# Sums of squares of a norm: channel groups added on VectorE in fp32 ahead of one column-sum matmul per half

## The reference

```python
def rms_norm(x, g):
    xf = x.astype(jnp.float32)
    y = xf * lax.rsqrt(jnp.mean(xf * xf, axis=-1, keepdims=True) + EPS)
    return (y * g.astype(jnp.float32)).astype(x.dtype)

h = modulate(rms_norm(x, g_ffn1), sh1, sc1);  x = x + 0.5 * gt1 * swiglu(h, w_ffn1_in, w_ffn1_out)
h = modulate(rms_norm(x, g_mix), sh2, sc2);   x = x + gt2 * token_mix(h, ...)
h = modulate(rms_norm(x, g_ffn2), sh3, sc3);  x = x + 0.5 * gt3 * swiglu(h, w_ffn2_in, w_ffn2_out)
```

## Time and profile before

| what | us |
|---|---|
| median of three runs | 1582.96 (1581.0 to 1584.09) |
| the profiled execution, its own time | 1581.47 |
| its span on the slowest core (spans of all: 1572.1 to 1579.6) | 1579.6 |
| TensorE matmul busy | 1494.0 (95%) |
| VectorE busy | 809.4 (51%) |
| ScalarE busy | 454.8 (29%) |
| GpSimd busy (it issues the weight loads) | 78.4 (5%) |
| chain that ended last, on TensorE | 88% of the span |

### The profile page before, as it was taken

How to read it: one execution, slowest core, us unless ns; L and a number is a source line. 1 busy time by engine, 2 the same in 40 slices (tenths; PEclk the granted TensorE clock), 3 DMA queues, 4 the chain that set the end, 5 groups by cost and what they waited for, 6 DMA issues and landing times.

```text
span 1579.6 us, 23368 instructions; the slowest of 8 cores (1572.1 to 1579.6 us)
## 1 busy us (share of the span) xinstructions
PE 1494.0 (95%) x8372; PEld 707.3 (45%) x8372; DVE 809.4 (51%) x1315; ACT 454.8 (29%) x641; POOL 78.4 (5%) x152
## 2 busy tenths in 40 slices
PE   1597999999999999988999999999999999999998
PEld 1243444444444444454565444444444444444443
DVE  1353717245163556667875557745544616253644
ACT  2462010110101026548666444523511010101010
POOL 1001000000000000000000000001000000000000
PEclk7799999999999999999999999999999999999999
DMA  9946142531624201340024445336332131211022
GB/s 176 249 84 94 29 71 47 88 67 28 107 54 74 41 14 67 76 103 1 15 68 73 76 68 121 68 64 116 54 54 40 28 54 28 47 27 28 1 107 107
DMA packets 24302, 107.12 MB, mean 68 GB/s; under 512 B 2816, under 2 KB 3072, under 8 KB 21760
## 3 DMA queue, kind: packets, MB, share of 16 engines
q0 software_dynamic: 21312, 75.67, 28.7%
q1 hardware_dynamic: 2880, 29.98, 5.4%
HBM read 168.71 MB, written 12.58 MB: 115 GB/s over the span
## 4 chain that ended last, share of the span: by engine, by line
PE 88%; DMA 6%; DVE 2%; ACT 2%; issue 2%; POOL 0%; DVEq 0%; ACTq 0%; POOLq 0%
PE ps L663 42%; PE ps L693 21%; PE ps L1007 7%; PE ps L817 4%; PE ps L1020 3%; PE ps L1039 3%; DMA arena<-w1i 2%; PE ps L953 1%; DMA arena<-w_kqvu 1%; PE ps L800 1%; PE ps L577 1%; DMA arena<-w_ada 1%; DVE arena L496 1%; PE ps L899 1%; PE ps L863 1%
## 5 line engine op out<-in xcount | busy, mean ns | idle before, releaser
L663 PE MATMUL ps<-arena 128*128 128x512 bf16 x3152 | 690.7, 380 | 7.8 <-DMA arena<-w1i 4.9
L484 ACT ACTIVATE arena<-ps 128x512 bf16<-128x512 f32 (+3 forms) x426 | 268.0, 653 | 967.1 <-PE ps L663 800.7
L663 PEld LDWEIGHTS ps<-arena 128*128 128x128 bf16 x3152 | 306.7, 98 | 376.9 <-issue 12.1
L496 DVE SCALAR_TENSOR_TENSOR arena<-ps,arena 128x512 f32<-128x512 f32 (+1 forms) x500 | 359.5, 747 | 79.0 <-PE ps L693 20.4
L490 DVE TENSOR_TENSOR arena<-arena,ps 128x512 bf16<-128x512 bf16 x198 | 134.7, 686 | 501.0 <-PE ps L663 482.4
L693 PE MATMUL ps<-arena 128*128 128x512 bf16 x1584 | 346.7, 380 | 5.9 <-DMA arena<-w1o 3.8
L693 PEld LDWEIGHTS ps<-arena 128*128 128x128 bf16 x1584 | 155.1, 98 | 194.1 <-issue 11.9
L490 DVE TENSOR_TENSOR arena<-arena 128x1024 bf16<-128x1024 bf16 (+8 forms) x178 | 109.9, 637 | 33.6 <-ACT arena L484 27.6
L1007 PE MATMUL ps<-arena 128*128 128x512 bf16 x512 | 116.0, 379 | 0.0
L496 DVE SCALAR_TENSOR_TENSOR arena<-arena 128x512 f32<-128x512 f32 (+1 forms) x120 | 84.4, 739 | 31.5 <-ACT arena L484 22.2
L484 ACT ACTIVATE arena<-arena 128x512 f32<-128x512 f32 (+2 forms) x86 | 89.5, 1053 | 35.7 <-DVE arena L496 22.8
(11 more groups left out here) (60 smaller groups left out, 495.5 us busy)
## 6 DMA issues: line engine op xcount, KB each, us to landing
arena<-w_ada POOLq DMA_DIRECT2D x36, 512.0 KB, 8.9
arena<-w_gate POOLq DMA_DIRECT2D x24, 512.0 KB, 7.3
arena<-w1i POOLq DMA_DIRECT2D x22, 512.0 KB, 7.1
arena<-w3i POOLq DMA_DIRECT2D x22, 512.0 KB, 5.2
arena<-x SPq DMA_DIRECT2D x5, 2048.0 KB, 14.1
outT<-arena SPq DMA_DIRECT2D x8, 1024.0 KB, 3.9
arena<-w1o POOLq DMA_DIRECT2D x10, 512.0 KB, 6.7
arena<-w_kqvu POOLq DMA_DIRECT2D x10, 512.0 KB, 7.9
```

Source lines behind the costliest of these rows:

```text
L484: return e.activation(out=o, in_=i, func=func, scale=scale)
L496: return e.scalar_tensor_tensor(out=out, in0=in0() if callable(in0) else in0, scalar=scalar, in1=in1() if callable(in1) else in1, op0=op0, ...
L663: ins = e.matmul(pst(t), lhsT=w[:, kt, :], rhs=hk(b, kt), start=(kt == 0), stop=(kt == 7))
```

## The change

`norm_stats` gets `sub` as an argument. ScalarE squares as before. For each half, VectorE adds the first two channel groups to the other two (bf16 in, fp32 out, 128 x 1024) into `pair`, which lies on the same bytes as the two buffers of `TMPS`; then it adds the two parts of `pair` (128 x 512) and writes bf16 into one of the two `SQK` buffers. TensorE then sums that over channels with one matmul per half, two per norm in place of eight. `kq_unit` takes the buffers of `SQK` in the same rotation, which now starts with the norms.

```diff
+    PAIRS = [view(o, F32, (2, TB)) for o in (o_qt, o_expb)]
...
     rk_pos = [0]
+    sqk_pos = [0]
     tmp_pos = [0]
 
-    def norm_stats(b):
+    def norm_stats(b, sub):
         t = Tile()
         for hf in range(2):
             sq = H[:, b, 4 * hf:4 * hf + 4, :]
             xs = xblk(b)[:, 4 * hf:4 * hf + 4, :]
             act(sq, xs, AF.Square, reads=[xs], writes=[sq], cost=1.88)
+        pair = PAIRS[0 if sub < 2 else 1]
         for hf in range(2):
-            sq = H[:, b, 4 * hf:4 * hf + 4, :]
-
-            def mm(e, hf=hf):
-                ins = None
-                for kt in range(4 * hf, 4 * hf + 4):
-                    ins = e.matmul(pst(t), lhsT=ONES, rhs=hk(b, kt), start=(kt == 0), stop=(kt == 7))
-                return ins
-            S.op("pe", mm, reads=[sq, ONES] + ([t] if hf else []), writes=[t], cost=mmc(4, 512))
+            sm = SQK[sqk_pos[0] % 2]
+            sqk_pos[0] += 1
+            lo, hi = H[:, b, 4 * hf:4 * hf + 2, :], H[:, b, 4 * hf + 2:4 * hf + 4, :]
+            tt(pair, lo, hi, ALU.add, [lo, hi], [pair], 1.15)
+            tt(sm, pair[:, 0, :], pair[:, 1, :], ALU.add, [pair], [sm], 0.62)
+            S.op("pe", lambda e, hf=hf, sm=sm: e.matmul(pst(t), lhsT=ONES, rhs=sm, start=(hf == 0), stop=(hf == 1)),
+                 reads=[sm, ONES] + ([t] if hf else []), writes=[t], cost=mmc(1, 512))
...
     def norm(b, sub):
-        norm_apply(b, sub, norm_stats(b))
+        norm_apply(b, sub, norm_stats(b, sub))
...
-    rs0 = norm_stats(0)
+    rs0 = norm_stats(0, 0)
...
-    sqk_pos = [0]
```

## The result

The changed kernel takes 1596.51 us (median of four runs, 1593.28 to 1599.22) against 1582.47 for the kernel before on the same chip (1581.0 to 1584.09). The ratio is 1.0089, with a 95% interval of 1.0072 to 1.0106: some 14 us slower. In some executions the cores of a die run at a lower granted clock (on one chip the kernel before took 1744 to 1869 us in them); every ratio here leaves these out. The forecast was 1577, 5.2 us faster by its sum, with a range up to 1587.

The account below looks back on a forecast made before the run. The prediction took mostly busy TensorE as the bound, the end moving with the second feed-forward step's start. Stages summed to -0.5 + 1.8 + 3.9 = 5.2 us earlier, 1577.8 on the median's scale, put at 1577; range 1566 to 1587.

Parts of the forecast that it names:

- What a norm costs and what it gives back: All norms: VectorE adds 3.83 us per norm, 53.6 in all; TensorE saves 1.3 per norm, ceiling 18.1.
- Sub 2: Stage 1004 to 1124 us: norm 1 gives 0, norms 2 to 4 give 1.3 each, 3.9 us earlier.
- Wait (2): Sub 2: the pair lies in the bias table, last read long before these norms' sums; no cost.
- Sub 1 up to the keys: Stage 561 to 687 us: norms 0 and 3 give 1.3 each, norm 2 loses 0.8; 1.8 us earlier.
- The stage of sub 0: 0 to 154 us: taken as 0.5 us later, bounds 5.2 earlier and 4.2 later.
- wait (1): Pair on `TMPS` bytes: a norm's first add waits for the previous norm's last temporary to be read; unit products wait too.
- the "+0.1": Sub 0, norm 2: 1.4 us later at the Silu batch, less 1.3 for norm 3's sums following at once.
- slower by the shared bytes: Rival: in five norms of sub 0 and 1 waiting adds block unit products, 12.7 us lost, 1588; chance 0.11.
- "Norm 4: ... 0": Sub 1, norm 4: its sums stand between a load's issue and the wait for it at 686.83; 0 gain.
- "no change, since priorities stay": 687 to 1004 us, where no norm runs: the planner reorders everything, but no change in time was taken.
- Wait (3): Key and query squares share `SQK` with the norms, but already waited for the last norm through `RK`; no cost.
- the planner loses what TensorE saves: Rival: a new order adds half as much idle time again in 687 to 1004 us, about 1583 to 1589; chance 0.08.

Follow-up runs that it names:

- after_order: Kernel before, its four sum matmuls per half and no adds, every queue in the order planned for the changed kernel: 1611.8 us, ratio 1.0191 to before.
- replay: Kernel before in its own planned order, in-place bf16 adds put in afterwards, one sum matmul per half: ratio 0.9980 to before.
- sub2_only: Kernel before with the new sums in the norms of sub 2 alone: ratio 0.9964 to before.
- sub1_only: Kernel before with the new sums in the norms of sub 1 alone: ratio 1.0056 to before.
- hybrid: Kernel before with the new sums only in norms 0 to 3 of sub 1 and in sub 2: ratio 0.9961 to before.
- own_pair: Changed kernel with `pair` on bytes that no norm's apply uses in that stage: ratio 1.0029 to the kernel before.
- after: The changed kernel itself, new sums in all norms: 1596.51 us, ratio 1.0089 to the kernel before.
- sub0_only: Kernel before with the new sums in the norms of sub 0 alone: ratio 1.0043 to before.
- short_adds: Changed kernel with the same plan but shortened adds, half of the squares left out of the sum: ratio 1.0073 to the kernel before.
- own_pair_sum: Changed kernel with `pair` on its own bytes and a separate sum buffer for the norms instead of `SQK`: ratio 0.9990 to the kernel before.
- inplace: Changed kernel with both adds in bf16, in place on the squares, without `pair` or `SQK`: ratio 1.0015 to the kernel before.
- the two with an early norm 4: Separate-bytes `pair` and in-place bf16 adds, each with planned priority for the adds of norm 4 of sub 1: ratios 0.9974 and 0.9984 to before.
- the replanned kernels: Kernel before, same work, planned cost of each half's four sum matmuls written as three or as one: ratios 1.0076 and 1.0026 to before.

## Why the prediction was wrong

**Right.** What a norm costs and what it gives back. The pair add took 1.222 us against 1.22, the small one 0.692 against 0.69, 53.6 in all as a term; VectorE's total rose by 50.8. The 1.3 us per norm agrees in sum with after_order against the change, 15 to 16 us. The page "VectorE: DVE Perf Modes" of the Trainium skill, section "What auto-detection actually checks", gives an add of two tensors its double rate only when every tensor is 16 bits wide. That held in both directions here: with an fp32 output the add of 1024 took 1.22 us, with bf16 throughout 0.688 (replay). Sub 2 was forecast 3.9 us earlier; sub2_only gained 5.7 by the ratio, and 4.2 in its own two columns. Wait (2), the bias table, shows nowhere: after 1004 us TensorE waits for 2.6 us in all on core 7, and not ahead of the sums.

**Right in number, not shown.** Sub 1 up to the keys was forecast 1.8 earlier, and that column is 1.4 shorter. But sub1_only, with the same norms changed, gains nothing in it (533.5), and hybrid is 0.6 longer (534.1). So the 1.4 can't be put down to the norms; the agreement may be luck.

**The stage of sub 0, mis-sized.** I had the mechanism, wait (1), with -0.5 us and bounds from 5.2 earlier to 4.2 later; it was 7.3 later. The step that failed is the sums of norm 3, in the "+0.1" at the end of norm 2's line. I followed norm 2's delay into the Silu batch (1.4 in the forecast, 1.5 measured: 96.08 for 94.60, though norm 2's Ln was 3.3 late, since TensorE now had units to do ahead of its sums), and let norm 3's sums "follow at once". They did not: norm 3's adds wait in turn for norm 2's last shift, the two halves come apart by the unit products between them, and TensorE, which before did all eight matmuls in one go, has 16 unit matmuls in front of the second half. The next line of the prediction names the same wait and "unit products between the adds" for norms 3 and 4, but gives them no price; the stage got 0.5 us in all. Norm 2's lateness cost nothing by itself: in own_pair it is as late, and the stage as short as before. The plans with the shared bytes (after, sub0_only, short_adds) lose 7.1 to 8.4 us there, those with the new sums and without these shared bytes (own_pair, own_pair_sum, inplace and the two with an early norm 4) from -0.2 to 4.0, so at least about half of the loss is theirs; the rest lies within what a mere new plan does there (3.6 and 5.4 in the replanned kernels). That the price isn't the length of the add is shown by short_adds; and after_order, 13.7 us longer there with no add in it, shows that the loss lies in the order. My rival "slower by the shared bytes" named these bytes, with 12.7 us for five norms and VectorE's queue in front of the unit products as the way; the 7.3 came at one norm and through the place of its second sum.

**"Norm 4: ... 0", and "no change, since priorities stay".** The larger loss. I put norm 4 of sub 1 at nothing since its sums lay under a wait for a load. That cover, 4.2 us long, was for TensorE's sums, which run beside VectorE. I didn't ask what is queued ahead of the adds on VectorE: the whole apply of norm 3, some 9 us. With the adds that late, the plan puts the sums behind the first keys on TensorE too, and the Ln of norm 4 came some 22 us later. The stretch from 687 to 1004 us, which the sum had at "no change, since priorities stay", became 16.8 us longer among keys and queries, 7.3 of them regained behind. The prediction asked "what waits behind it" of each add, and not what it waits behind.

**Wait (3), "they already waited for the last norm through `RK`. No cost."** The first key square needed nothing of norm 4 before: at 690.50 it ran as soon as its keys were there. Through `SQK` it now waits for the sum of norm 4 (9.56 and 10.39 us of ScalarE's idle time end with that sum). I had looked at the wait for `RK` two instructions later and not that for the square itself. As a reading that was wrong; as a price it was nearly right: after_order has no such wait, its first key square comes 3.9 us behind the keys' first matmul as before, and the stretch is still 171.2 us, with 1.3 us more of norm 4's sums in it. So the wait itself is worth some 2 us of the 172.0, by that run.

**The rival of the planner.** I gave "the planner loses what TensorE saves" 0.08, on the ground that priorities stay. The runs show what a new plan alone can do: 4.1 and 12.0 us for the same instructions with one planned cost changed. The forecast's gain of 5.2 was of that size, so a forecast of its sign needed a chance for the order of about equal weight, and the range had to be wider by some 10 us upward. Also, both rivals came at once. I had added each to the other norms' gains, so that none reached 1596; shared bytes (7.3) and the late norm 4 (some 10) have different places, and nothing kept them from adding up. The prediction's own last sign of being wrong, another order in 687 to 1004 us that moves the second step by more than the norms do, is what came.

**Open.** How the late apply of norm 4 turns into some 10 us, step by step through keys and queries: part is a lower granted clock (0.94 for 0.97), and the rest isn't taken apart here. How much of the 7.3 us in the first weight group the shared bytes cause and how much is chance of the plan. And whether another planned cost for the adds would have given a good order by luck: the two replanned kernels show only that the spread is of this size.

What beats both kernels is the change without the places where it lost: hybrid, 0.39% faster than before (0.25 to 0.53) and, by the two ratios, 1.3% faster than the change. sub2_only does as well.

## What to carry to other kernels

When work moves from an engine that is full to one that has room, ask at each place what stands in front of it in that engine's queue, not only what will stand behind it, and where the work that waits for it will then stand in its own queue: an average of 51% busy said nothing about the 9 us ahead of norm 4. A scratch buffer that is reused across stages carries a wait with it, and a chain of such waits must be walked to its end. In a kernel whose order a planner makes, first measure what a new plan with the same work costs; a gain smaller than that can't be forecast from the work alone.

## What the chip showed beside that

Short gaps of TensorE stood ahead of a fall of its clock, which cost more time than any one of them. In the key and query stretch after, core 7, five pieces of 785 to 810 us, in the columns of the earlier trace rows:

```profile
785.00:790.00 5.00, 3.88 (x37) 1.76 (x33) 3.96 (x9) 3.98 (x7) 0.00 (x0) 1.00 0.01 2
790.00:795.00 5.00, 3.09 (x39) 1.46 (x39) 4.31 (x10) 4.46 (x7) 0.00 (x0) 0.86 0.01 3
795.00:800.00 5.00, 3.26 (x32) 1.84 (x33) 4.21 (x9) 2.19 (x3) 0.00 (x0) 0.50 0.00 0
800.00:805.00 5.00, 5.00 (x42) 2.67 (x41) 2.74 (x7) 1.24 (x3) 0.00 (x0) 0.62 0.00 0
805.00:810.00 5.00, 5.00 (x31) 2.11 (x29) 3.97 (x10) 4.14 (x7) 0.00 (x0) 1.00 0.02 5
```

TensorE pauses for up to 1.0 us at a time, for ScalarE and VectorE, from 788 us on; the granted clock falls to 0.50, the lower of the two levels (1.2 GHz for 2.4), and is back at 1.00 from 805 us, after 5 us in which TensorE was busy throughout. Eight matmuls at the lower level and eight shortly after it:

```profile
799.25 3.60 PE L818 MATMUL ps<-arena 128*128 128x512 bf16 x8
...
806.89 1.90 PE L818 MATMUL ps<-arena 128*128 128x512 bf16 x8
```

Time at the lower level shows as busy time. That is one reason why TensorE's busy time fell by 4.7 to 9.7 us only, where I had written 18: in the key and query stretch it rose by 11.4, of which the 30 more matmuls, moved there from the next stretch, are 6.5 at 0.2158 us each. The other 4.9 go with the lower clock, 0.94 for 0.97; I haven't taken them apart further.

And two adds of which the second needs the first's result are 0.17 us apart on VectorE, which I hadn't priced; this one is the second add of norm 3, whose first, at 94.94, took 1.23:

```profile
96.34 0.69 DVE L491 TENSOR_TENSOR arena<-arena 128x512 bf16<-128x512 f32 x1 [0.17 <-DVE arena L491]
```
